# Feed-forward activations turned on VectorE in 32x32 blocks instead of on TensorE, and one low part per group moved to GpSimd

## The chip, the cores and the metric

The kernel runs on one core of one Trainium2 chip. The time is the device time of one execution in microseconds (us); lower is better. A comparison of this kernel with itself resolves differences of about 0.2%, that is some 6 us.

## What is computed

A block of 256 tokens with 2048 channels goes through feed-forward, token mixing (three kinds of attention), feed-forward again, and then two more layers with four mixers each. Everything is float32. What matters here are the two feed-forward parts:

```python
def _swiglu(h, w_gu, w_down):          # h 256 x 2048, w_gu 2048 x 11264, w_down 5632 x 2048
    gate, up = jnp.split(h @ w_gu, 2, axis=-1)
    return (jax.nn.silu(gate) * up) @ w_down

x = x + 0.5 * _swiglu(_rmsnorm(x, ffn1_norm), ffn1_w_gu, ffn1_w_down)
x = x + _token_mixing(_rmsnorm(x, mix_norm), ...)
x = x + 0.5 * _swiglu(_rmsnorm(x, ffn2_norm), ffn2_w_gu, ffn2_w_down)
```

In the second block each layer also needs `mod = silu(c) @ w_ada + b_ada` for one row `c`, with `w_ada` 2048 x 6144. It does not depend on `x`, and the kernel works it out during the feed-forward parts (called "ada" below).

## The kernel before

**Weights as slabs.** All weights stream from memory in slabs of 512 KB, one after another, in one fixed order that all engines share. SyncE starts the transfers (`load`, L693) into four buffers (`stage`). A float32 weight is used as the sum of two rounded parts: ScalarE writes the high part (`rounded_part`, L1411), and then either VectorE (`slab_lo`, L1830) or GpSimd (`rest`, L777) writes the low part, stage minus high. The set `by_vector` says who makes the low part of which slab. In the feed-forward parts it holds the odd slabs and GpSimd has the even ones. There are four places for split slabs too: ScalarE may round slab n once TensorE has finished slab n-4, and SyncE may load slab n+4 once the low part of slab n is written.

**TensorE** (`wide_passes`) does twelve matmuls of 512 columns on a slab: eight with the high part of the weight (L898), for which it waits for ScalarE, and then four with the low part (L903), for which it waits for VectorE or GpSimd.

**One group** of a feed-forward part is 16 slabs, eight for 512 gate columns and eight for 512 up columns. There are 11 groups (j = 0 to 10) and then 88 slabs of the down projection. Slab q of group j is called (j, q) here. Around a group's end the products are made into the input of the down projection:
- ScalarE, at (j, 11): `silu` of the gate product, from PSUM into the tile SILU (L1472), 128 tokens x 512 channels, twice.
- VectorE, at (j+1, 3): `gated` multiplies by the up product (L1876, two instructions).
- TensorE, after (j+1, 2): `turn_act` turns the tile with eight 128x128 transposes (L816) into PSUM banks 6 and 7, since the down projection needs channels on partitions.
- ScalarE, at (j+1, 6): `round_act` writes the high part of the turned tile (L1478, two instructions).
- VectorE, at (j+1, 7): `rest_act` writes the low part (L1884, two instructions). The down projection waits for `act_lo`.

For j = 10 these steps fall in the first slabs of the down projection, which stand in as a group 11.

**Order on VectorE.** Every engine goes through its own list in order. VectorE's list at a slab is: the low part if the slab is its own, then `ada_pick` if due, then one `ada` step if due, then `rest_act` or others. An ada step (L1843 or L1840, then L1846) adds two rows of `w_ada` chunks of 512 columns; there are 96 of them in each feed-forward part, one on every 2.4 slabs from slab 18 to slab 245. After each eighth one TensorE sums over partitions (`ada_reduce`, L957), one slab later, and VectorE picks the result (`ada_pick`, L1857 and L1858), one more slab later. So at a pick VectorE stands still until TensorE has come to that very slab. By `ADA_AT` the picks fall on (2, 4), (3, 7), (4, 11), (5, 14), (7, 1), (8, 4), (9, 7), (10, 10) and (11, 14), and three later in the down projection.

## Time and profile before

| | |
|---|---|
| time, median of 3 runs | 3107.89 us (3107.75 to 3108.13) |
| span of the profiled execution | 3105.2 us |
| TensorE busy | 3070.2 us, 99% |
| VectorE busy | 1952.8 us, 63% |
| ScalarE busy | 1447.7 us, 47% |
| GpSimd busy | 1270.0 us, 41% |
| TensorE clock granted | full in all 40 slices |

The profile is one execution seen by the hardware profiler. Its span is 2.7 us below the median time, since the time also counts what lies before the first and after the last instruction. A busy time contains the time in which an instruction has started and is held up. The chain is followed back from the last instruction to whatever released each step. The first feed-forward part runs from the start to about 755 us, the second from about 1475 to 2214 us.

### The profile page before, as it was taken

What the parts mean: (1) busy time and instruction counts of PE and PEld (TensorE: products, weight loads), DVE (VectorE), ACT (ScalarE), POOL (GpSimd) and SP (SyncE); (2) the same over time, 40 slices, a digit from 0 to 9 for tenths busy, and PEclk for the clock granted to TensorE, in tenths of its full rate; (3) what the DMA queues carried; (4) which work ended last, traced back from release to release, by engine and by line L of the source; (5) the groups of instructions that cost most, each with busy time, mean ns of one, the idle gap of its engine ahead of it and who ended that gap; (6) DMA issues with size and microseconds to landing.
All of it is one profiled execution on the core that took longest, in us unless ns stands there. A gap on an engine that the chain in (4) does not pass through costs nothing.

```text
span 3105.2 us, 46479 instructions
## 1 busy us (share of the span) xinstructions
PE 3070.2 (99%) x19038; PEld 2713.0 (87%) x19038; DVE 1952.8 (63%) x2398; ACT 1447.7 (47%) x1877; POOL 1270.0 (41%) x621
## 2 busy tenths in 40 slices
PE   8999999999999999999999999999999999999998
PEld 7888888888999999998888888888899998899986
DVE  5778576673323446773467667677469864589764
ACT  6444444444567545544544444344444454544444
POOL 4444444444566554584444444444610004510013
PEclk9999999999999999999999999999999999999999
DMA  7878777785776565565787778787666545565454
GB/s 230 284 245 282 260 268 268 252 283 175 218 177 181 156 168 145 150 172 195 237 270 257 273 252 276 244 290 246 191 181 190 158 142 199 166 191 178 155 166 166
DMA packets 486653, 662.74 MB, mean 213 GB/s; under 512 B 67992, under 2 KB 273544, under 8 KB 486184
## 3 DMA queue, kind: packets, MB, share of 16 engines
q1 hardware_dynamic: 480952, 655.05, 66.1%
q0 software_dynamic: 4448, 2.94, 0.4%
q8 instruction: 150, 2.46, 0.3%
q10 hardware_dynamic: 1040, 1.78, 0.2%
q14 instruction: 63, 0.52, 0.1%
HBM read 655.47 MB, written 2.10 MB: 212 GB/s over the span
## 4 chain that ended last, share of the span: by engine, by line
PE 97%; DVE 1%; ACT 1%; issue 0%; DMA 0%; POOL 0%; ACTq 0%; DVEq 0%
PE ps L898 36%; PE ps L826 23%; PE ps L903 18%; PE ps L832 11%; PE ps L816 2%; PE ps L857 1%; PE ps L1356 1%; PE ps L1144 1%; PE ps L1125 1%; PE ps L957 0%; PE ps L1052 0%; PE ps L1152 0%; PE ps L1182 0%; PE ps L1174 0%; PE ps L1191 0%
## 5 line engine op out<-in xcount | busy, mean ns | idle before, releaser
L777 POOL TENSOR_TENSOR split_slabs<-stage,split_slabs 128x1024 fp32r<-128x1024 f32 x296 | 749.8, 2534 | 1365.6 <-ACT split_slabs L1411 1365.6
L1411 ACT ACTIVATE split_slabs<-stage 128x1024 fp32r<-128x1024 f32 x592 | 627.6, 1062 | 903.7 <-PE ps L903 665.1
L898 PE MATMUL ps<-split_slabs,h_split 128*128 128x512 f32 x3312 | 827.1, 392 | 0.9 <-ACT split_slabs L1411 0.9
L1411 ACT ACTIVATE narrow_split_slabs<-stage 128x1024 fp32r<-128x1024 f32 (+1 forms) x440 | 461.0, 1052 | 651.2 <-PE ps L832 568.1
L826 PE MATMUL ps<-h_split,narrow_split_slabs 128*128 128x256 f32 x5856 | 748.4, 280 | 0.0
L898 PEld LDWEIGHTS ps<-split_slabs,h_split 128*128 128x128 f32 x3312 | 620.8, 188 | 133.8 <-issue 5.1
L826 PEld LDWEIGHTS ps<-h_split,narrow_split_slabs 128*128 128x128 f32 x5856 | 702.8, 188 | 15.7 <-issue 12.0
L1830 DVE TENSOR_TENSOR split_slabs<-stage,split_slabs 128x1024 fp32r<-128x1024 f32 x296 | 412.2, 1395 | 368.2 <-ACT split_slabs L1411 368.1
L777 POOL TENSOR_TENSOR narrow_split_slabs<-stage,narrow_split_slabs 128x1024 fp32r<-128x1024 f32 (+1 forms) x181 | 436.0, 2418 | 315.0 <-ACT narrow_split_slabs L1411 307.3
L1830 DVE TENSOR_TENSOR narrow_split_slabs<-stage,narrow_split_slabs 128x1024 fp32r<-128x1024 f32 x259 | 333.1, 1288 | 175.8 <-ACT narrow_split_slabs L1411 174.9
L903 PE MATMUL ps<-split_slabs,h_split 128*128 128x512 f32 x1656 | 443.0, 389 | 0.3 <-POOL split_slabs L777 0.3
L832 PE MATMUL ps<-h_split,narrow_split_slabs 128*128 128x256 f32 x2928 | 397.8, 278 | 1.6 <-POOL narrow_split_slabs L777 1.4
L903 PEld LDWEIGHTS ps<-split_slabs,h_split 128*128 128x128 f32 x1656 | 310.9, 188 | 65.9 <-POOL split_slabs L777 0.7
L832 PEld LDWEIGHTS ps<-h_split,narrow_split_slabs 128*128 128x128 f32 x2928 | 364.2, 188 | 2.6 <-POOL narrow_split_slabs L777 2.0
L898 PE MATMUL ps<-split_slabs,act_split 128*128 128x512 f32 x1392 | 344.6, 390 | 0.0
L898 PEld LDWEIGHTS ps<-split_slabs,act_split 128*128 128x128 f32 x1392 | 260.9, 188 | 54.2
L1843 DVE SCALAR_TENSOR_TENSOR U<-U,cact 128x512 f32<-128x512 f32 x168 | 213.6, 1271 | 5.1 <-DMA U<-in_w_ada 4.7
L1846 DVE SCALAR_TENSOR_TENSOR U<-U,cact 128x512 f32<-128x512 f32 x192 | 201.3, 1048 | 6.8
L903 PE MATMUL ps<-split_slabs,act_split 128*128 128x512 f32 x696 | 186.1, 389 | 0.0
L903 PEld LDWEIGHTS ps<-split_slabs,act_split 128*128 128x128 f32 x696 | 130.6, 188 | 27.4
L1857 DVE TENSOR_TENSOR ps<-ps,base_consts 128x512 f32<-128x512 f32 x24 | 16.8, 700 | 162.1 <-PE ps L957 162.1
L2191 DVE SCALAR_TENSOR_TENSOR U<-U,params 128x256 f32<-128x256 f32 x240 | 110.8, 503 | 0.0
(250 smaller groups left out, 2129.4 us busy)
## 6 DMA issues: line engine op xcount, KB each, us to landing
stage<-in_w_in SPq DMA_DIRECT2D x360, 512.0 KB, 3.7
stage<-in_ffn_w_gu SPq DMA_DIRECT2D x352, 512.0 KB, 4.8
U<-in_w_ada SPq DMA_DIRECT2D x192, 512.0 KB, 5.6
stage<-in_ffn_w_down SPq DMA_DIRECT2D x176, 512.0 KB, 5.6
stage<-in_w_out SPq DMA_DIRECT2D x96, 512.0 KB, 4.1
stage<-in_w_in SPq DMA_DIRECT2D x80, 128.0 KB, 2.9
stage<-in_w_branch_c SPq DMA_DIRECT2D x32, 192.0 KB, 3.3
stage<-in_cmp_w SPq DMA_DIRECT2D x8, 512.0 KB, 5.8
```

The source lines that it names most:

```text
L777: nc.gpsimd.tensor_tensor(slab_part(n, 1, size(n)), stage[:, n % RING, 0:size(n)], slab_part(n, 0, size(n)).bitcast(F32), ALU.subtract).th ...
L816: return nc.tensor.transpose(dst, src, ident[0:n, 0:n])
L826: mm(bank[:, c * S:(c + 1) * S], w[0][:, kk, at:at + P], moving(kk, i), start=first and c == 0 and kk == 0 and i == 0, stop=False)
L832: ins = mm(bank[:, c * S:(c + 1) * S], w[1][:, kk, at:at + P], moving(kk, 0), start=False, stop=last and c == outs - 1 and kk == chunks - 1)
L857: ins = mm(acc(g)[:, c * S:(c + 1) * S], w[:, kk, c * P:(c + 1) * P], hx[:, i, KC * k + kk, :], start=first and c == 0 and kk == 0, stop=l ...
L898: mm(ps[:, 2 * pair + T, :], stationary(kk, i)[:, T * P:(T + 1) * P], w[0][:, kk, :], start=first and kk == 0 and i == 0, stop=False)
L903: ins = mm(ps[:, 2 * pair + T, :], stationary(kk, 0)[:, T * P:(T + 1) * P], w[1][:, kk, :], start=False, stop=last and kk == WK - 1)
L1411: return fn(slab_part(n, 0, size(n)), stage[:, n % RING, 0:size(n)], ACT.Copy)
L1830: v.tensor_tensor(slab_part(n, 1), stage[:, n % RING, :], slab_part(n, 0).bitcast(F32), ALU.subtract).then_inc(lo_vec, 1)
L1843: ins = v.scalar_tensor_tensor(total, w[:, 0, :], cact[:, 2 * k:2 * k + 1], total, ALU.mult, ALU.add)
L1846: v.scalar_tensor_tensor(total, w[:, 1, :], cact[:, 2 * k + 1:2 * k + 2], total, ALU.mult, ALU.add).then_inc(ada_load, 1)
L2191: ins = v.scalar_tensor_tensor(cy[:, c, :], src, col, cy[:, c, :], ALU.mult, ALU.add)
```

## The change

The eight transposes and the PSUM banks go away. VectorE turns the tile itself: a vector transpose works inside blocks of 32x32, and here each instruction reads 32 partitions (one quadrant `a`) and writes 32 partitions (quadrant `b`), 256 elements on each, so that 16 instructions place all blocks where a full transpose needs them. They are put on VectorE's list four at a time, at (j+1, 4) to (j+1, 7). The turned tile lies where the low part will be; ScalarE rounds it from there in one instruction of 1024 elements, at (j+1, 10), and VectorE writes the low part over it in one instruction, at (j+1, 11). TensorE no longer waits for anything of this. Slab (j, 5) of the groups 1 to 11 goes from VectorE to GpSimd.

```diff
+        def turned_act(j):
+            return u(AT - SHIFT + FC * S + 4 * j * S, P, 4 * S)
...
+        by_vector -= {s + 16 * j + 5 for s in (S_F1, S_F2) for j in range(1, GU_GROUPS + 1)}
...
-            def turn_act(f, j):
-                at = GU_GROUPS * f + j
-                pe.wait_ge(evacuated, (G_F1, G_F2)[f] + j + 1)
-                if at == 0:
-                    pe.wait_ge(*vec_out.after("par", len(PARAM_TILES) - 1))
-                if at > 0:
-                    pe.wait_ge(act_lo, at)
-                for c in range(4):
-                    for T in range(TT):
-                        last = transpose(ps[:, 6 + c // 2, (c % 2) * S + T * P:(c % 2) * S + (T + 1) * P],
-                                         u(SILU, P, TT, WN)[:, T, c * P:(c + 1) * P])
-                last.then_inc(act_turned, 1)
...
-                            if side == 0 and q == 2 and j > 0:
-                                turn_act(f, j - 1)
...
             def round_act(f, j):
                 act.wait_ge(act_turned, GU_GROUPS * f + j + 1)
-                for k in range(2):
-                    fn(ats[:, 0, (4 * j + 2 * k) * S:(4 * j + 2 * k + 2) * S], ps[:, 6 + k, :], ACT.Copy).then_inc(act_hi, 1)
+                part = slice(4 * j * S, 4 * (j + 1) * S)
+                fn(ats[:, 0, part], turned_act(j), ACT.Copy).then_inc(act_hi, 1)
...
-                        if j > 0 and q == 6:
+                        if j > 0 and q == 10:
                             round_act(f, j - 1)
...
+                def turn_act(j, a):
+                    rows = slice(a * SQUARE, (a + 1) * SQUARE)
+                    src = u(SILU, P, TT, WN).rearrange("p t (c w) -> p t c w", c=4)
+                    dst = turned_act(j).rearrange("p (c t s) -> p t c s", c=4, t=TT)
+                    if a == 0:
+                        dve.wait_ge(evacuated, g0 + j + 1)
+                    for b in range(P // SQUARE):
+                        turned_rows = slice(b * SQUARE, (b + 1) * SQUARE)
+                        last = v.transpose(dst[turned_rows, :, :, rows], src[rows, :, :, turned_rows])
+                    if a == P // SQUARE - 1:
+                        last.then_inc(act_turned, 1)
+
                 def rest_act(j):
-                    at = GU_GROUPS * f + j
-                    for k in range(2):
-                        part = slice((4 * j + 2 * k) * S, (4 * j + 2 * k + 2) * S)
-                        dve.wait_ge(act_hi, 2 * at + k + 1)
-                        last = v.tensor_tensor(ats[:, 1, part], ps[:, 6 + k, :], ats[:, 0, part].bitcast(F32), ALU.subtract)
-                    last.then_inc(act_lo, 1)
+                    part = slice(4 * j * S, 4 * (j + 1) * S)
+                    dve.wait_ge(act_hi, GU_GROUPS * f + j + 1)
+                    v.tensor_tensor(ats[:, 1, part], turned_act(j), ats[:, 0, part].bitcast(F32), ALU.subtract
+                                    ).then_inc(act_lo, 1)
...
-                        if j > 0 and q == 7:
+                        if j > 0 and 4 <= q < 8:
+                            turn_act(j - 1, q - 4)
+                        if j > 0 and q == 11:
                             rest_act(j - 1)
```

## Rows read from the trace of the kernel before

**Rows 1.** The page: busy times, and the chain that ended last by engine.
```profile
PE 3070.2 (99%) x19038; PEld 2713.0 (87%) x19038; DVE 1952.8 (63%) x2398; ACT 1447.7 (47%) x1877; POOL 1270.0 (41%) x621
...
PE 97%; DVE 1%; ACT 1%; issue 0%; DMA 0%; POOL 0%; ACTq 0%; DVEq 0%
```
**Rows 2.** Chain in order of time: start us, us, what; around one turning, first part.
```profile
67.07 1.81 PE ps L898 x8
68.88 0.91 PE ps L903 x4
69.79 0.87 PE ps L816 x8
70.67 1.84 PE ps L898 x8
```
**Rows 3.** Timeline of TensorE (start us, us, what) around the turning in group 7.
```profile
337.81 1.07 PE L903 MATMUL ps<-split_slabs,h_split 128*128 128x512 f32 x4
339.01 1.09 PE L816 MATMUL ps<-base_consts,U 128*128 128x128 f32 x8
```
**Rows 4.** Single lines, whole span: count, shortest/median/longest ns, first and last start.
```profile
L1884 DVE TENSOR_TENSOR act_split<-ps,act_split x44: 676/681/687, 77.0 to 1988.0; 128x512 fp32r<-128x512 f32 x44
...
L1830 DVE TENSOR_TENSOR split_slabs<-stage,split_slabs x296: 1207/1224/3457, 27.5 to 3086.5; 128x1024 fp32r<-128x1024 f32 x148
...
L1843 DVE SCALAR_TENSOR_TENSOR U<-U,cact x168: 735/746/2978, 69.6 to 2156.1; 128x512 f32<-128x512 f32 x168
...
L1840 DVE TENSOR_SCALAR U<-U,cact x24: 476/481/2625, 62.1 to 2117.1; 128x512 f32<-128x512 f32 x24
...
L2273 DVE COPY U<-ps x16: 412/418/422, 2377.9 to 2987.4; 128x256 f32<-128x256 f32 x16
...
L777 POOL TENSOR_TENSOR split_slabs<-stage,split_slabs x296: 2375/2402/3495, 11.6 to 3082.9; 128x1024 fp32r<-128x1024 f32 x148
```
**Rows 5.** Timelines of VectorE and GpSimd in group 7.
```profile
340.79 2.77 DVE L1846 SCALAR_TENSOR_TENSOR U<-U,cact 128x512 f32<-128x512 f32 x1
...
346.06 1.22 DVE L1830 TENSOR_TENSOR split_slabs<-stage,split_slabs 128x1024 fp32r<-128x1024 f32 x1
347.20 1.28 DVE L1884 TENSOR_TENSOR act_split<-ps,act_split 128x512 fp32r<-128x512 f32 x2
...
340.40 2.62 POOL L777 TENSOR_TENSOR split_slabs<-stage,split_slabs 128x1024 fp32r<-128x1024 f32 x1 [3.83 <-ACT split_slabs L1411]
347.06 2.48 POOL L777 TENSOR_TENSOR split_slabs<-stage,split_slabs 128x1024 fp32r<-128x1024 f32 x1 [4.05 <-ACT split_slabs L1411]
```
**Rows 6.** Busy time of each engine in stretches from one turning to the next.
```profile
115.10:160.00 44.90, 44.90 (x203) 37.21 (x203) 36.77 (x35) 18.98 (x21) 20.49 (x8) 1.00 0.84 285
...
340.10:384.50 44.40, 44.40 (x202) 36.82 (x201) 27.16 (x28) 19.02 (x21) 19.77 (x8) 1.00 0.86 294
...
sum 448.60, PE 448.47 PEld 371.50 DVE 322.96 ACT 190.78 POOL 204.35; mean PE 44.85 PEld 37.15 DVE 32.30 ACT 19.08 POOL 20.44
```
**Rows 7.** What VectorE waited for from 60 to 550 us: total us, times, longest.
```profile
DVE split_slabs L1830 <- ACT split_slabs L1411: 71.8, 33, 4.4
DVE ps L1857 <- PE ps L957: 60.4, 9, 8.5
```
**Rows 8.** Timeline of VectorE and chain of TensorE after the pick at (2, 4).
```profile
118.34 0.70 DVE L1857 TENSOR_TENSOR ps<-ps,base_consts 128x512 f32<-128x512 f32 x1 [4.85 <-PE ps L957]
...
122.00 1.22 DVE L1830 TENSOR_TENSOR split_slabs<-stage,split_slabs 128x1024 fp32r<-128x1024 f32 x1
...
127.92 1.22 DVE L1830 TENSOR_TENSOR split_slabs<-stage,split_slabs 128x1024 fp32r<-128x1024 f32 x1
...
126.51 1.81 PE ps L898 x8
...
131.95 1.81 PE ps L898 x8
```

More of the change, by code:

```diff
@@ L44 @@
 SHIFT = 16
+SQUARE = 32
 GU_GROUPS, DOWN_GROUPS = FF // WN, D // WN
@@ L1015, in ffn @@
                             wide_passes(PAIR[g1 + d], n, act_, q == 0, q == DOWN - 1)
-                        if d == 0 and q == 2:
-                            turn_act(f, GU_GROUPS - 1)
                         if f == 0 and d > 0 and q == 6:
@@ L1512, in ffn_act @@
                     round_upto(s0 + GU_SLABS + i)
-                    if i == 6:
+                    if i == 10:
                         round_act(f, GU_GROUPS - 1)
@@ L1928, in ffn_vec @@
                     between(GU_SLABS + i)
-                    if i == 7:
+                    if 4 <= i < 8:
+                        turn_act(GU_GROUPS - 1, i - 4)
+                    if i == 11:
                         rest_act(GU_GROUPS - 1)
```

## The prediction, made before the changed kernel was run

> **What bounds the kernel now.** I read the page first: busy times, then the chain that ended last. TensorE is busy 99% of the span and holds 97% of the chain [rows 1]. The reader should see that nothing else carries weight: as long as the low and high parts of the slabs come in time, the time is the sum of what TensorE is given, and whatever is taken off it comes off the time. The second view is the chain in order of time around one turning. A slab is 1.81 + 0.91 = 2.72 us, and between two slabs stand 0.87 us of transposes [rows 2]. The third question is what keeps the slabs coming. For that I read the stretches from one turning to the next, the waits of VectorE, and the timelines of VectorE and GpSimd side by side [rows 4 to 8].
>
> **What is removed.** 22 turnings (11 in each feed-forward part) go from TensorE. Each costs 0.87 us, and the eight matmuls behind it take 1.84 instead of 1.81 us [rows 2], so 0.90 us each: 22 x 0.90 = 19.8 us, all on the path. In group 7 the turning started late as well: the four matmuls before it started at 337.81, so it was due 0.91 us later [rows 2], at 338.72, and started at 339.01 [rows 3]. It waited for `gated`. That happens in both parts, since the order is the same: 2 x 0.3 = 0.6 us, also gone. Sum: 20.4 us. The two PSUM banks that come free are used by nobody else here, and TensorE's clock is at full in every slice, so it gives or costs nothing.
>
> ScalarE rounds 1024 elements in one instruction instead of two of 512: nothing, it is busy 19 of 45 us [rows 6]. If its wait for `act_turned` comes late, the high parts of slabs (j, 11) and (j, 12) and the next `silu` are queued behind it; this is taken up below.
>
> **What is added on VectorE.** The trace shows no vector transpose. The nearest row for one instruction is a copy of 256 elements, one input, at 418 ns [rows 4]. Two independent instructions overlap by some 0.08 us (two of 681 ns in 1.28 us [rows 4, 5]), so the bounds for the pace are 0.34 us (they overlap) and, if a transpose takes two cycles for an element, the 418 ns plus once more the difference that 256 elements make: 681 - 418 = 263 ns, so 0.70 us. I take 0.45 us, no overlap: 1.8 us for each of the four parts and 7.2 us a group (bounds 5.5 and 11.2). The Trainium skill (VectorE: DVE Perf Modes, "Two Vector instructions with no wait between them") says that an instruction whose output starts in another quadrant than the last output is held until all earlier ones have finished. Every one of these sixteen writes another quadrant than the one before; by that rule the pace is the 0.45 us, and without it 0.34 us; no row here has such a pair.
>
> Off VectorE's list come one low part in a group, 1.13 us where its neighbours follow at once, and the old `rest_act`, 1.28 us; the new one is one instruction of 1024 elements from SBUF, 1.2 us. Net +6.0 us a group. GpSimd gets one more low part of 2.4 us [rows 4], 9 instead of 8 in a group, 21.6 of 44 us. Slabs 4, 5 and 6 are then all its own; one comes every 2.72 us and takes 2.40, so it keeps up if it is not held.
>
> **What of this is covered.** Idle time on VectorE is 44.85 - 32.30 = 12.6 us a group on average, but only 8.1 us in the stretch from 115 us, and 17 us in the one from 340 us [rows 6]. So 6 us fit on average. But two things make the cover thinner than it looks. First, of 138 idle us about 60 stand before a pick [rows 7]. They are lead that is thrown away: at a pick VectorE meets TensorE at the same slab and has to rebuild its lead. Second, VectorE and GpSimd exclude each other. A scalar_tensor_tensor with two inputs in SBUF, normally 0.75 us, took 2.77 us because GpSimd had started 0.4 us before it, and ended just after GpSimd did; while `rest_act` of before, with one input in PSUM, ran straight through a GpSimd instruction in 1.28 us for two [rows 5]. The longest and shortest times say the same for the whole span: 676 to 687 ns for L1884, but up to 3457 and 2978 ns for L1830 and L1843, and GpSimd's own up to 3495 [rows 4]. The new `rest_act` reads two inputs from SBUF and joins those that can be held.
>
> So I follow the list after a pick. TensorE needs the low part of slab n 1.81 us after the slab's start. At (2, 4): the low part of slab 7 was ready at 123.2 and needed at 126.51 + 1.81 = 128.3, margin 5.1; that of slab 9 at 129.1 and 133.8, margin 4.6 [rows 8]. In the new order three parts of the turning come before slab 7 and the low part of slab 5 is gone: 5.4 - 1.1 = 4.3 later, margin 0.8. Before slab 9 come four parts, and `rest_act` is gone: 7.2 - 1.1 - 1.3 = 4.8 later, margin -0.2. At (7, 1): the low part of slab 7 was ready at 347.3 [rows 5] and needed at 340.10 + 4 x 2.72 + 1.81 = 352.8; 4.3 later, and needed 1.2 us earlier since the turning and its wait are gone from before it: margin 0.0. Each can be hit by one GpSimd instruction, 0 to 2.4 us. ScalarE's rounding of the turned tile comes about 5 us into slab 7 in such a group, and the high part of slab 11 behind it has some 2 us to spare. I give each of these places half a GpSimd instruction, 1.2 us. They are (2, 4), (7, 1) and (8, 4) in each of the two parts, six places: 7.2 us. The picks at slab 7 (groups 3 and 9) change little, as 1.8 us replaces the old 1.28 us there, and the other groups keep margins of 1 to 3 us: together 0.6 us. Sum of new stalls 7.8 us, between 0 and, with a full GpSimd instruction and a negative margin at each place and half that in four others, 6 x 2.6 + 4 x 1.2 = 20 us.
>
> The sum: 3105.2 - 20.4 + 7.8 = 3092.6 us of span, and with the 2.7 us around it 3095.3 us, against a median of 3107.9.
>
> **The rivals.** *The cover holds:* the transposes overlap at 0.34 us, so that every margin above grows by over 1 us, and the collisions fall elsewhere. For it: in the group from 340 us VectorE has 17 idle us. Against: the margins of slabs 7 and 9. Time: 3107.9 - 20.4 = 3087.5.
>
> *The stalls eat the gain:* 20 us of stalls as bounded above, 3107.5. For it: GpSimd's extra 2.4 us falls on just the stretch where VectorE is behind, and GpSimd and VectorE together had little free time in the stretch from 115 us, 36.8 + 20.5 us of 44.9 with what they wait for each other [rows 6]. Against: a stall of TensorE gives all others that time, so it can't repeat at once.
>
> *The transpose is slow and VectorE becomes the bound:* at 0.70 us the turning takes 11.2 us a group, 4.0 more. The six margins fall by 3 to 4 us each, 6 x 3.5 = 21 us, and those of 1 to 3 us in some ten other groups turn to stalls of about 1 us: 3095.3 + 31 = 3126. It decides from about 0.55 us for an instruction.
>
> *The transpose takes part in the exclusion:* this is the one on the other side with the greatest price. The instruction has one input, in SBUF. The tensor_scalar L1840 has also one, does 512 elements in 481 ns, clearly more than an element in the time that L1843 needs for one (746 ns), and it too was held up to 2625 ns [rows 4]. If the transpose is such a fast form, time that can't be shared in a group is GpSimd 9 x 2.4 = 21.6, low parts 7 x 1.1, ada 6.7 x 1.2 (0.75 less some 0.15 in which an instruction is only starting, twice), 1 for its split, 1.1 for `rest_act` and 5 for the transposes: 44.4 us of the 43.9 that a group would have, before any wait for each other. With the 5 us that neither uses in front of the picks, a group is some 4 us longer, over 20 groups 80 us: 3167. It decides if the sixteen together take over about 3 us of the shared time. The Trainium skill (SBUF — State Buffer, "Who interferes with whom") lists copy, cast and tensor_scalar as forms that take the shared ports, and says that a VectorE instruction with at most one SBUF input outside these modes does not contend; transposes are not in its list. L1840 and L1884 here agree with both halves of it, and no row has a transpose; by the rule this rival falls away.
>
> **How the numbers follow.** Some stalls, 3095.3: 0.52. Cover holds, 3087.5: 0.17. Stalls eat the gain, about 3102 to 3110: 0.13. Slow transpose, 3126: 0.10. Exclusion, 3167: 0.08. About 0.2% (6 us) is what a measurement can tell, so faster means below 3101.7. Faster 0.69, same 0.13, slower 0.18. The range holds the first three: from 3086 (all of the 20.4 us and a little rounding) to 3112.
>
> **What would show it.** L816 falls from 614 to 438 instructions and the chain around slab (j, 2) runs 2.72 us after 2.72 us. The transposes are 352 in two stretches, with a mean near 0.42 us; about 0.3 with a longest over 2 means the exclusion, 0.7 the slow one. Right if the waits of TensorE show a few us in total for low parts by VectorE or GpSimd, at slabs 7 and 9 after the picks in groups 2, 7 and 8, and VectorE's busy time in a group rises from 32 to about 39 us. Wrong if these waits are near nothing (cover holds) or appear in all groups.

## The result, and the profile after

The changed kernel takes 3115.45 us (median of 20 runs, 3106.57 to 3125.36) where the kernel before takes 3108.01 us (20 runs, 3102.73 to 3112.01): ratio 1.0025, with a 95% interval of 1.0018 to 1.0031. Forecast were 3095.3 us and a range up to 3112. The median lies above the range, and the sign is wrong. The profiled execution is one of 3111.67 us, with a span of 3109.8 us, against 3105.2 before.

The page of the kernel after, busy times and shares of the chain by engine:

```profile
PE 3056.2 (98%) x18862; PEld 2695.1 (87%) x18862; DVE 2151.5 (69%) x2706; ACT 1445.6 (46%) x1855; POOL 1354.0 (44%) x643
...
PE 89%; DVE 7%; issue 1%; DMA 1%; ACT 1%; POOL 0%; ACTq 0%; DVEq 0%
```

Against [rows 1], TensorE is busy 14 us less and still the bound, but the chain is now 7% VectorE: there are places where TensorE stands and VectorE is what it stands for. TensorE's waits in the feed-forward parts (us in total, times, longest):

```profile
PE ps L910 <- DVE split_slabs L1819: 17.6, 10, 3.8
PE ps L964 <- DVE ada_split L1839: 0.8, 1, 0.8
```

L910 is the four matmuls with the low part, and L1819 the low part by VectorE. Such a wait comes right after eight matmuls with the high part. The first is in group 1, in which there is no pick. TensorE's timeline there (start, length, line, operation, count, idle time before it with its releaser):

```profile
79.44 1.98 PE L905 MATMUL ps<-split_slabs,h_split 128*128 128x512 f32 x8
84.36 1.71 PE L910 MATMUL ps<-split_slabs,h_split 128*128 128x512 f32 x4 [2.95 <-DVE split_slabs L1819]
85.87 3.10 PE L905 MATMUL ps<-split_slabs,h_split 128*128 128x512 f32 x8
88.80 1.07 PE L910 MATMUL ps<-split_slabs,h_split 128*128 128x512 f32 x4
```

Two things cost time here. TensorE is idle for 2.95 us, and the twelve matmuls after it run from 84.36 to 88.80, 4.44 us, where a slab's twelve took 2.72 before [rows 2]. Why the second is so shows in the window over them (length; busy time of PE, PEld, DVE, ACT and POOL with counts; granted clock of TensorE; DMA share; GB/s):

```profile
84.40:87.00 2.60, 2.60 (x7) 2.06 (x8) 2.53 (x5) 0.84 (x1) 0.00 (x0) 0.58 0.56 117
...
50.00:100.00 50.00, 47.05 (x203) 38.30 (x202) 42.31 (x45) 22.14 (x25) 26.13 (x10) 0.97 0.70 237
200.00:250.00 50.00, 47.09 (x200) 38.29 (x199) 44.49 (x50) 19.20 (x19) 22.60 (x10) 0.97 0.68 230
350.00:400.00 50.00, 47.09 (x196) 38.42 (x195) 37.78 (x43) 20.25 (x20) 24.02 (x10) 0.93 0.78 269
1800.00:1850.00 50.00, 45.55 (x193) 36.90 (x192) 48.10 (x49) 18.88 (x20) 23.51 (x9) 0.97 0.74 254
```

After the stall the granted clock is at the lower of its two levels (1.2 instead of 2.4 GHz), here for 3.4 us and in the window from 350 us for 6.8. In this execution it followed each of the four stalls of 2.9 us or more (at 84, 225, 362 and 1822 us), and none of the shorter ones, of which the longest is 2.41 us. Other runs show that the length of the stall alone doesn't decide it. In slab5_back (below) the clock fell behind a stall of 2.39 us and not behind one of 3.18 us; these are the windows right after the two:

```profile
178.00:182.00 4.00, 4.00 (x12) 3.13 (x11) 3.83 (x8) 1.06 (x1) 0.00 (x0) 0.57 0.77 249
...
565.00:572.00 7.00, 6.52 (x28) 5.36 (x29) 5.15 (x8) 2.12 (x2) 0.12 (x1) 1.00 0.48 151
```

The cost in the kernel after is read from the windows of 50 us around its four long stalls, the share of the clock that was not granted times their length: (0.03 + 0.03 + 0.07 + 0.03) x 50 = 8 us.

**Where the time went.** I cut each trace at the same three instructions: the first matmul of the mixing, the first wide one of the second feed-forward part, the last of that part.

| us | first feed-forward | mixing | second feed-forward | two layers |
|---|---|---|---|---|
| before | 755.2 | 723.4 | 735.5 | 891.1 |
| after | 764.0 | 724.5 | 734.4 | 886.9 |

The two feed-forward parts together grew by 7.7 us, although 20.4 us of work was taken off them (below this is measured to be right). So 28.1 us came in: 18.4 in waits, 8 by the clock, and 1.7 not placed. The last column differs by up to 8 us between runs whose code there is the same (886.9 us here, 895 in before_log_later), so the feed-forward columns tell more than the total.

**What holds VectorE.** Its timeline in group 1 ahead of that stall, and GpSimd's:

```profile
65.72 3.19 DVE L1819 TENSOR_TENSOR split_slabs<-stage,split_slabs 128x1024 fp32r<-128x1024 f32 x1
...
68.84 2.88 DVE L1832 SCALAR_TENSOR_TENSOR U<-U,cact 128x512 f32<-128x512 f32 x1
71.76 2.78 DVE L1835 SCALAR_TENSOR_TENSOR U<-U,cact 128x512 f32<-128x512 f32 x1
74.46 3.57 DVE L1879 STREAM_TRANSPOSE U<-U 32x256 f32<-32x256 f32 x8
...
79.62 1.78 DVE L1879 STREAM_TRANSPOSE U<-U 32x256 f32<-32x256 f32 x4
81.42 2.89 DVE L1819 TENSOR_TENSOR split_slabs<-stage,split_slabs 128x1024 fp32r<-128x1024 f32 x1
```

```profile
65.44 2.39 POOL L784 TENSOR_TENSOR split_slabs<-stage,split_slabs 128x1024 fp32r<-128x1024 f32 x1 [2.02 <-ACT split_slabs L1400]
68.36 5.62 POOL L784 TENSOR_TENSOR split_slabs<-stage,split_slabs 128x1024 fp32r<-128x1024 f32 x2 [0.53 <-ACT split_slabs L1400]
...
80.88 2.35 POOL L784 TENSOR_TENSOR split_slabs<-stage,split_slabs 128x1024 fp32r<-128x1024 f32 x1 [3.08 <-ACT split_slabs L1400]
```

Both halves of an ada step, 0.75 us each when free, take 2.88 and 2.78 us, each together with a GpSimd instruction. Two holds in a row cost 4.2 us, the transposes come that much later, and the low part at 81.42, late already, is held once more (2.89 us instead of 1.22): TensorE gets it 2.95 us late. Over the whole span (count: shortest/median/longest in ns; stretch):

```profile
L1879 DVE STREAM_TRANSPOSE U<-U x352: 422/436/443, 74.5 to 2004.8; 32x256 f32<-32x256 f32 x176
L1832 DVE SCALAR_TENSOR_TENSOR U<-U,cact x168: 734/747/2906, 68.8 to 2164.9; 128x512 f32<-128x512 f32 x168
L1835 DVE SCALAR_TENSOR_TENSOR U<-U,cact x192: 750/752/2955, 63.7 to 2165.6; 128x512 f32<-128x512 f32 x192
L1819 DVE TENSOR_TENSOR split_slabs<-stage,split_slabs x274: 1208/1224/3426, 26.5 to 3091.1; 128x1024 fp32r<-128x1024 f32 x137
L1886 DVE TENSOR_TENSOR act_split<-U,act_split x22: 1215/1221/3434, 93.4 to 2009.0; 128x1024 fp32r<-128x1024 f32 x22
L1970 DVE TENSOR_SCALAR U<-U x8: 181/181/2280, 153.0 to 253.2; 128x32 f32<-128x32 f32 x8
L1969 DVE TENSOR_TENSOR U<-U x8: 187/192/2391, 152.7 to 253.0; 128x32 f32<-128x32 f32 x8
```

The transposes are never held and never slow. Held are, of these rows, the instructions with two inputs in SBUF and the `tensor_scalar`. L1886 is the new `rest_act`. The rows of L1969 and L1970 were not in my working at all: they belong to `log_sigmoid`, a small part of the mixing that VectorE makes ahead of time in groups 2 to 6 of the first feed-forward part, at (j, 1). They take 0.19 us, and when held up to 2.4.

The kernel before has such holds too, with nearly as much time in them. These are the first instruction of an ada step in the kernel before and in the kernel after (busy us, mean ns), against a median of 0.75 us in both:

```profile
L1843 DVE SCALAR_TENSOR_TENSOR U<-U,cact 128x512 f32<-128x512 f32 x168 | 213.6, 1271 | 5.1 <-DMA U<-in_w_ada 4.7
```

```profile
L1832 DVE SCALAR_TENSOR_TENSOR U<-U,cact 128x512 f32<-128x512 f32 x168 | 225.0, 1339 | 11.3 <-DMA U<-in_w_ada 10.7
```

So the holds are not new. What is new is that TensorE has to wait behind some of them.

### The profile page after: what moved, and what is told of

Same layout as the page of the kernel before. It is cut to its first block, busy times and chain, and to the rows that moved or that the text cites. A ratio compares the mean times of both kernels' runs of the same rounds, so it can differ in the third digit from the quotient of the medians.

```text
span 3109.8 us, 46413 instructions
## 1 busy us (share of the span) xinstructions
PE 3056.2 (98%) x18862; PEld 2695.1 (87%) x18862; DVE 2151.5 (69%) x2706; ACT 1445.6 (46%) x1855; POOL 1354.0 (44%) x643
## 4 chain that ended last, share of the span: by engine, by line
PE 89%; DVE 7%; issue 1%; DMA 1%; ACT 1%; POOL 0%; ACTq 0%; DVEq 0%
PE ps L905 31%; PE ps L833 23%; PE ps L910 16%; PE ps L839 11%; PE ps L823 2%; DVE split_slabs L1819 1%; DVE U L1832 1%; DVE U L1879 1%; PE ps L864 1%; DVE U L1835 1%; PE ps L1345 1%; PE ps L1133 1%; PE ps L1114 1%; POOL narrow_split_slabs L784 0%; DMA stage<-in_ffn_w_gu 0%
## 5 line engine op out<-in xcount | busy, mean ns | idle before, releaser
L784 POOL TENSOR_TENSOR split_slabs<-stage,split_slabs 128x1024 fp32r<-128x1024 f32 x318 | 834.7, 2628 | 1283.9 <-ACT split_slabs L1400 1283.6
L1819 DVE TENSOR_TENSOR split_slabs<-stage,split_slabs 128x1024 fp32r<-128x1024 f32 x274 | 406.5, 1486 | 238.5 <-ACT split_slabs L1400 237.7
L910 PE MATMUL ps<-split_slabs,h_split 128*128 128x512 f32 x1656 | 447.5, 392 | 16.3 <-DVE split_slabs L1819 16.0
L1819 DVE TENSOR_TENSOR narrow_split_slabs<-stage,narrow_split_slabs 128x1024 fp32r<-128x1024 f32 x259 | 332.3, 1285 | 171.4 <-ACT narrow_split_slabs L1400 170.1
L910 PEld LDWEIGHTS ps<-split_slabs,h_split 128*128 128x128 f32 x1656 | 311.9, 189 | 85.3 <-DVE split_slabs L1819 19.7
L1832 DVE SCALAR_TENSOR_TENSOR U<-U,cact 128x512 f32<-128x512 f32 x168 | 225.0, 1339 | 11.3 <-DMA U<-in_w_ada 10.7
L1835 DVE SCALAR_TENSOR_TENSOR U<-U,cact 128x512 f32<-128x512 f32 x192 | 221.7, 1155 | 6.8
L910 PE MATMUL ps<-split_slabs,act_split 128*128 128x512 f32 x696 | 186.5, 390 | 1.6 <-DVE split_slabs L1819 1.6
L1879 DVE STREAM_TRANSPOSE U<-U 32x256 f32<-32x256 f32 x352 | 153.2, 435 | 5.3
L910 PEld LDWEIGHTS ps<-split_slabs,act_split 128*128 128x128 f32 x696 | 130.4, 188 | 30.0 <-DVE split_slabs L1819 2.9
```

The lines of the kernel that those rows point to most:

```text
L784: nc.gpsimd.tensor_tensor(slab_part(n, 1, size(n)), stage[:, n % RING, 0:size(n)], slab_part(n, 0, size(n)).bitcast(F32), ALU.subtract).th ...
L910: ins = mm(ps[:, 2 * pair + T, :], stationary(kk, 0)[:, T * P:(T + 1) * P], w[1][:, kk, :], start=False, stop=last and kk == WK - 1)
L1819: v.tensor_tensor(slab_part(n, 1), stage[:, n % RING, :], slab_part(n, 0).bitcast(F32), ALU.subtract).then_inc(lo_vec, 1)
L1832: ins = v.scalar_tensor_tensor(total, w[:, 0, :], cact[:, 2 * k:2 * k + 1], total, ALU.mult, ALU.add)
L1835: v.scalar_tensor_tensor(total, w[:, 1, :], cact[:, 2 * k + 1:2 * k + 2], total, ALU.mult, ALU.add).then_inc(ada_load, 1)
L1879: last = v.transpose(dst[turned_rows, :, :, rows], src[rows, :, :, turned_rows])
```

## The experiments

Each ratio is to runs of the kernel before on the same chip, with its 95% interval.

### Is GpSimd's extra low part the cause?

**slab5_back**, the kernel after with slab (j, 5) given back to VectorE:

```diff
-        by_vector -= {s + 16 * j + 5 for s in (S_F1, S_F2) for j in range(1, GU_GROUPS + 1)}
```

> The changed kernel with one part undone: the low part of slab (j, 5) goes back from GpSimd to VectorE; the transposes stay on VectorE. Theory X (the stalls come from VectorE being held by GpSimd, and the extra GpSimd instruction makes slabs 4, 5 and 6 one row of three holds just where the turning is): the waits of TensorE for low parts by VectorE fall from 17.6 us to under 6 us, and the time to 3092 to 3100 us. Theory Y (the stalls come from the turning's own 7.2 us on VectorE's list; GpSimd is incidental): VectorE has 1.1 us more in front of slab 7, so the waits are 17 us or more and the time 3113 to 3125 us.

Measured: 3122.89 us (3121.56 to 3125.98, 5 runs), ratio 1.0046 (1.0034 to 1.0058). TensorE's wait for the low parts by VectorE:

```profile
PE ps L909 <- DVE split_slabs L1818: 23.9, 19, 3.9
```

The waits grow from 17.6 to 23.9 us, as theory Y expected. I had seen the extra GpSimd instruction as the one that VectorE meets; it is a relief of about 7 us: without it VectorE has 1.2 us more on its list in front of slab 7.

**slab5_alone**, the kernel before with that one line added.

> The kernel before, with only the low part of slab (j, 5) given to GpSimd; the transposes stay on TensorE. Theory X: the row of three GpSimd instructions by itself eats most of the margin of slabs 7 and 9, TensorE waits 4 to 10 us in total for low parts, 3112 to 3120 us. Theory Y: VectorE has less to do, no waits, 3108 us as before (within 2).

Measured: 3106.97 us (3102.55 to 3112.49, 11 runs), ratio 0.9995 (0.9987 to 1.0004). Alone, this half of the change does nothing. It does give holds in a row, as theory X said. In group 1 of slab5_alone:

```profile
70.59 2.89 DVE L1844 SCALAR_TENSOR_TENSOR U<-U,cact 128x512 f32<-128x512 f32 x1
73.51 2.77 DVE L1847 SCALAR_TENSOR_TENSOR U<-U,cact 128x512 f32<-128x512 f32 x1
```

Ada steps with both halves held (over 1.3 us each, one right behind the other) are found 20 times in the feed-forward parts of slab5_alone, 10 times in the kernel after, and never in the kernel before or in slab5_back. They come with GpSimd's extra low part. But slab5_alone has them and no stall, and slab5_back has none and more waits, so they are not what decides.

### What is the removed work worth, and does VectorE's extra time eat it?

**four_wide_turns**, the kernel after with four transposes over 128 partitions instead of sixteen over 32 (it leaves out the moves between quadrants):

```diff
-                    for b in range(P // SQUARE):
-                        turned_rows = slice(b * SQUARE, (b + 1) * SQUARE)
-                        last = v.transpose(dst[turned_rows, :, :, rows], src[rows, :, :, turned_rows])
+                    last = v.transpose(dst[:, :, :, rows], src[:, :, :, rows])
```

> The changed kernel with the sixteen transposes of a turning replaced by four over all 128 partitions (each turns the blocks inside every quadrant, so the blocks do not move between quadrants: this part of the computation is left out). VectorE has 1.8 instead of 7.2 us for a turning, all else is as in the changed kernel, GpSimd's extra low part too. Both theories: 3087 to 3090 us if the removal from TensorE is worth the 20.4 us that was worked out. Theory X in its strong form (the row of three GpSimd instructions is enough) expects 4 to 8 us of waits left, 3092 to 3098 us; theory Y none.

Measured: 3087.61 us (3084.32 to 3091.76, 5 runs), ratio 0.9935 (0.9923 to 0.9948). TensorE's waits for low parts by VectorE, the first turning on VectorE's timeline, and the same row of the ada steps as above:

```profile
PE ps L910 <- DVE split_slabs L1819: 0.9, 2, 0.5
...
68.92 2.88 DVE L1832 SCALAR_TENSOR_TENSOR U<-U,cact 128x512 f32<-128x512 f32 x1
71.84 2.77 DVE L1835 SCALAR_TENSOR_TENSOR U<-U,cact 128x512 f32<-128x512 f32 x1
74.53 0.76 DVE L1877 STREAM_TRANSPOSE U<-U 128x256 f32<-128x256 f32 x2
...
75.96 2.77 DVE L1835 SCALAR_TENSOR_TENSOR U<-U,cact 128x512 f32<-128x512 f32 x1
...
L1832 DVE SCALAR_TENSOR_TENSOR U<-U,cact 128x512 f32<-128x512 f32 x168 | 255.1, 1518 | 15.8 <-DMA U<-in_w_ada 15.3
```

The feed-forward parts take 744.4 + 726.0 = 1470.4 us, 20.3 less than before: the 20.4 us of the forecast are all there once VectorE has 5.5 us a group less to do. The granted clock in them is at full. So the whole loss comes through VectorE's list. The holds are all still there: the same two in front of the first turning, one more behind it, and a mean of 1518 ns for the ada instruction, more than the 1339 of the kernel after. Held this much, VectorE still keeps up when the turning is 5.5 us shorter. The stalls need the length of the turning as well as the holds.

### Ada steps away from the turning, and log-sigmoid away from the groups

**ada_aside**, the kernel after with no ada step on slabs 3 to 7 of a group:

```diff
-ADA_AT = [18 + m * 230 // ADA_LOADS for m in range(ADA_LOADS)]
+ADA_FREE = [i for i in range(18, 249) if not (i < 16 * 12 and 3 <= i % 16 <= 7)]
+ADA_AT = [ADA_FREE[m * (len(ADA_FREE) - 3) // (ADA_LOADS - 1)] for m in range(ADA_LOADS)]
```

> The changed kernel with the ada steps moved: none falls on slabs 3 to 7 of the groups 1 to 11, so nothing stands on VectorE's list there but gated, the turning and the low parts of slabs 3 and 7. About 3 us (two steps, more when held) leave the stretch in front of slab 7. Both theories expect fewer stalls; X, for which each ada step is two chances to be held for up to 2.4 us, expects nearly none, 3088 to 3094 us; Y expects about half of them left, 3098 to 3106 us.

Measured: 3112.06 us (3099.7 to 3116.01, 12 runs), ratio 1.0005 (0.9994 to 1.0015), which neither theory had expected. The waits are still 15.2 us, but two of them, 5.09 and 4.67 us, stand right behind `log_sigmoid`, at slab 3 of the groups 3 and 5 (in this order group 5 also has a pick at slab 1). VectorE and GpSimd of this kernel in group 3:

```profile
151.92 0.19 DVE L1970 TENSOR_TENSOR U<-U 128x32 f32<-128x32 f32 x1
152.14 2.36 DVE L1971 TENSOR_SCALAR U<-U 128x32 f32<-128x32 f32 x1
154.54 0.19 DVE L1970 TENSOR_TENSOR U<-U 128x32 f32<-128x32 f32 x1
154.76 2.33 DVE L1971 TENSOR_SCALAR U<-U 128x32 f32<-128x32 f32 x1
157.13 2.32 DVE L1970 TENSOR_TENSOR U<-U 128x32 f32<-128x32 f32 x1
159.49 2.25 DVE L1971 TENSOR_SCALAR U<-U 128x32 f32<-128x32 f32 x1
...
154.64 7.06 POOL L785 TENSOR_TENSOR split_slabs<-stage,split_slabs 128x1024 fp32r<-128x1024 f32 x3 [0.18 <-ACT split_slabs L1401]
```

Four holds in six instructions. As long as GpSimd has low parts waiting, each of VectorE's tiny instructions that can be held may meet another GpSimd instruction. The price of such a step on VectorE's list is therefore not its length alone, but also how many times it gives way.

**log_later**, the kernel after with `log_sigmoid` in the down projection instead (slabs 74 to 82, its scratch tile in memory of its own):

```diff
-                        if f == 0 and 2 <= j < 7 and q == 1:
-                            log_sigmoid(j - 2)
...
+                    if f == 0 and 74 <= i < 84 and i % 2 == 0:
+                        log_sigmoid(i // 2 - 37)
```

> The changed kernel with the log-sigmoid of the decay logits moved: some thirty VectorE instructions of 32 elements, 0.19 us each, at (2, 1) to (6, 1) of the first feed-forward part, go to slabs 74 to 82 of its down projection, where no ada step and no turning is left (their scratch gets a place of its own). Theory Z (VectorE stalls TensorE where it is behind, and each instruction with SBUF operands, however short, is then held for a whole GpSimd instruction): the stalls of the first part become like those of the second, 764 us for it become 752 to 757, and the time 3103 to 3109 us. Rival (short instructions do not matter, their own 6 us over five groups is all): first part 760 to 763, time 3112 to 3115.

Measured: 3107.76 us (3101.21 to 3114.93, 11 runs), ratio 0.9995 (0.9984 to 1.0006); the first feed-forward part falls from 764.0 to 754.6 us, and the waits from 17.6 to 12.2 us. The stalls of 2.41 and 2.91 us at slab 7 of the groups 3 and 4 are gone, each with a `log_sigmoid` at slab 1 of its group before. So this explains 9 us (0.30% between the two ratios), and why the first part suffered more than the second.

**before_log_later**, the kernel before with the same move.

> The kernel before with the same move of the log-sigmoid and nothing else. All theories: no stall of TensorE depends on it, 3106 to 3110 us, as the kernel before.

Measured: 3110.44 us (3103.93 to 3113.86, 11 runs), ratio 0.9996 (0.9987 to 1.0005). Before the change `log_sigmoid` cost nothing where it stood; only with the turning on VectorE does it cost something.

**ada_aside_log_later**, both moves in the kernel after.

> Both moves: ada steps off the slabs 3 to 7, log-sigmoid in the down projection. With the ada steps moved the two stalls of 5 us that were left in the first part each stood behind a log-sigmoid whose short instructions were held 2.3 us apiece. Theory Z: each part is then 4 to 7 us shorter than before the change, 3094 to 3101 us, waits of TensorE for VectorE under 6 us. Rival (VectorE is simply full and the stall comes elsewhere): 3104 to 3110.

Measured: 3098.45 us (3096.88 to 3102.72, 5 runs), ratio 0.9963 (0.995 to 0.9975). **two_slabs_more** gives GpSimd slab (j, 9) as well:

```diff
-        by_vector -= {s + 16 * j + 5 for s in (S_F1, S_F2) for j in range(1, GU_GROUPS + 1)}
+        by_vector -= {s + 16 * j + q for q in (5, 9) for s in (S_F1, S_F2) for j in range(1, GU_GROUPS + 1)}
```

> As the one with both moves, and the low part of slab (j, 9) given to GpSimd as well. If VectorE's own load is what is left (slab 5 on VectorE had cost 7 us): 3088 to 3095 us. If GpSimd's holds weigh as much as the load they relieve: no better, 3096 to 3102.

Measured: 3102.47 us (3096.84 to 3107.56, 9 runs), ratio 0.9976 (0.9967 to 0.9986). The waits of the two kernels, first ada_aside_log_later:

```profile
PE ps L912 <- DVE split_slabs L1821: 5.5, 11, 1.4
```

and two_slabs_more:

```profile
PE ps L912 <- DVE split_slabs L1821: 10.0, 13, 3.0
```

With both moves no stall is longer than 1.4 us, and the clock of the feed-forward parts is at full; the feed-forward parts take 1482.1 us, 8.6 less than before. One low part more to GpSimd gains nothing. Whether it costs something isn't shown: the two intervals overlap, and its profile is of the slowest of its nine runs.

**before_ada_aside_log_later** is the control, the kernel before with both moves.

> The kernel before (transposes on TensorE) with the two moves of the version at 3098 us: ada steps off the slabs 3 to 7 of the groups, log-sigmoid in the down projection. If the gain of that version comes from taking the transposes off TensorE: 3108 to 3116 us here (nothing to gain from the moves; a few us lost where the down projection has more ada steps, as the waits at 600 to 690 us there showed). If the moves gain by themselves: below 3103.

Measured: 3118.26 us (3110.93 to 3122.86, 9 runs), ratio 1.0032 (1.0021 to 1.0043). In this order of the work the turning change, with its extra low part, is worth 1.0032 - 0.9963 = 0.69% or 21 us, all that was forecast for the removal. The order itself costs the kernel before 10 us, a little more than was expected (up to 3116 us).

### Does the order of the ada steps cost by itself?

Three kernels with `log_sigmoid` moved and the ada steps at fixed slabs of each group: **ada_even_log_later** (from after), **ada_even_slab5_back** (the same with slab 5 given back) and **before_ada_even_log_later** (from before).

```diff
-ADA_AT = [18 + m * 230 // ADA_LOADS for m in range(ADA_LOADS)]
+ADA_SLOTS = (0, 1, 8, 10, 11, 13, 15)
+ADA_AT = [i for i in range(18, 16 * 12) if i % 16 in ADA_SLOTS]
+ADA_AT += [16 * 12 + 1 + m * 54 // (ADA_LOADS - len(ADA_AT)) for m in range(ADA_LOADS - len(ADA_AT))]
```

> The changed kernel with the log-sigmoid in the down projection and the ada steps on fixed places of each group, seven at slabs 0, 1, 8, 10, 11, 13 and 15 of the groups 1 to 11 and the other 21 evenly over the down projection. In the version before it nine of sixteen slabs of the down projection's first part had an ada step and most of the waits that were left stood there. If VectorE's momentary backlog is what sets the waits: under 3 us of waits for low parts, 3090 to 3097 us. If not, as there, 3098 (3096 to 3101).

> The same with the low part of slab (j, 5) back on VectorE. In the changed kernel that step cost 7 us. If it is VectorE's own load against the margin of slabs 7 and 9, the margin is now 3 us and more, since no ada step stands there, and 1.1 us of it does no harm: within 3 us of the run beside it. If GpSimd's extra instruction is a relief at any place: 5 to 8 us slower again.

> The kernel before (transposes on TensorE) with the same two moves. TensorE never waited for low parts there, so the moves can gain nothing: 3107 to 3111 us, as the kernel before. If it came out below 3103, the gain of the other runs would be the moves' own and not that of taking the transposes off TensorE.

Measured: 3138.51 us (6 runs), ratio 1.0096 (1.0079 to 1.0112); 3139.4 (6 runs), 1.0093 (1.0078 to 1.0107); 3143.79 (5 runs), 1.0108 (1.0094 to 1.0121). All three are some 30 us slower than the kernel before and miss what was expected, the one from before as well, so it isn't the turning. SyncE's queue points to the cause (before_ada_even_log_later):

```profile
SPq L705 <- DVE U L1849: 415.8, 113, 10.5
```

and the kernel before:

```profile
SPq L702 <- DVE U L1846: 97.3, 63, 6.1
```

The loads of ada weights and of slabs go through one queue in one order. An ada load waits for one of two buffers. The reading is that with two steps on neighbouring slabs it waits longer, and the slab loads behind it wait too. By `ADA_AT` there are 31 such pairs here and none in the kernel before; the order of ada_aside has 16, and its cost in the kernel before was 10 us. These three say nothing on the holds.

**ada_every_second** takes the pairs away:

```diff
-ADA_AT = [18 + m * 230 // ADA_LOADS for m in range(ADA_LOADS)]
+ADA_AT = [i for i in range(18, 16 * 12) if i % 16 in (0, 2, 8, 10, 12, 14)]
+ADA_AT += [16 * 12 + 1 + m * 62 // (ADA_LOADS - len(ADA_AT)) for m in range(ADA_LOADS - len(ADA_AT))]
```

> The changed kernel with the log-sigmoid in the down projection and ada steps never on neighbouring slabs: slabs 0, 2, 8, 10, 12 and 14 of each group, then every second slab of the down projection. The version with pairs (10 and 11; 15, 0 and 1) lost 30 us with and without the turning on VectorE. If pairs are what was wrong there: 3093 to 3099 us. If any fixed list that keeps slabs 3 to 7 free and is denser elsewhere loses: 3110 or more.

Measured: 3112.78 us (3107.8 to 3117.12, 11 runs), ratio 1.0011 (1.0003 to 1.002). Most of the 30 us are gone with the pairs (this order also has six instead of seven steps in a group, so the pairs are not the only difference). The time is in the range of the second expectation, though it is slower than log_later by only some 5 us. It has five stalls, four of 3.0 us and one of 2.6. The four stand in the groups 5 and 9 of both parts, at the low part of slab 3, one slab behind the picks of this order on (5, 2) and (9, 2). So here the lead that is lost at a pick does show.

### The same work on VectorE without the holds of the ada steps

If the stalls need the holds, they must go when VectorE does the same work without being held. [rows 5] show how: an instruction with an input in PSUM runs through a GpSimd instruction. **ada_sum_in_psum** is the kernel after with the running sum of the ada steps in PSUM bank 5, which is free in these parts (the squares of the norm, whose output nobody reads, go to SBUF there):

```diff
-                w, total = u(ADA_RING, P, 2, WK, WN)[:, m % 2], u(ADA_ACC + WN, P, WN)
+                w, total = u(ADA_RING, P, 2, WK, WN)[:, m % 2], ps[:, 5, :]
...
```

> The changed kernel with the running sum of the ada steps in PSUM bank 5 instead of SBUF (ScalarE's unused squares go to SBUF for that). Each ada instruction then has one SBUF input and takes the same time by itself. Theory E (what breaks VectorE's margins is being held by GpSimd through two-input SBUF instructions): the 360 ada instructions, median 0.75 us and longest 2.9 us before, now all take under 0.8 us, VectorE's busy time falls by 60 to 150 us, waits of TensorE for low parts by VectorE fall from 17.6 us to under 6, time 3092 to 3100 us. Theory L (it is the own length of the list): ada instructions are not shorter in the median, waits stay above 12 us, time 3110 to 3118 us.

Measured: **3087.66 us (3086.96 to 3091.1, 5 runs), ratio 0.9929 (0.9916 to 0.9941)**, faster than both kernels. Its page, its ada steps and the window from 60 to 550 us:

```profile
PE 3049.4 (99%) x18862; PEld 2694.5 (87%) x18862; DVE 1934.9 (63%) x2706; ACT 1445.0 (47%) x1855; POOL 1316.9 (43%) x643
...
L1833 DVE SCALAR_TENSOR_TENSOR ps<-U,cact,ps x168: 704/749/758, 67.0 to 2139.6; 128x512 f32<-128x512 f32 x168
L1836 DVE SCALAR_TENSOR_TENSOR ps<-U,cact,ps x192: 754/756/758, 63.0 to 2140.4; 128x512 f32<-128x512 f32 x192
...
60.00:550.00 490.00, 489.76 (x2159) 404.95 (x2158) 370.11 (x495) 209.21 (x209) 255.20 (x101) 1.00 0.80 270
```

and the same window of the kernel after, then of the kernel before:

```profile
60.00:550.00 490.00, 477.70 (x2072) 392.34 (x2071) 439.03 (x483) 203.47 (x202) 263.03 (x98) 0.99 0.77 262
```

```profile
60.00:550.00 490.00, 489.87 (x2204) 405.86 (x2203) 347.25 (x334) 207.37 (x218) 225.66 (x89) 1.00 0.79 267
```

The same 2706 instructions on VectorE are busy 2151.5 - 1934.9 = 217 us less. The medians of these two rows differ by 4 ns at most from those of the kernel after, so nearly all of it was time in which instructions stood. No ada step goes above 758 ns. The picks, the log-sigmoid, the turning and GpSimd's list are where they were in the kernel after, and yet in the window TensorE is idle for 0.2 us, at full clock. The feed-forward parts take 1470.6 us, 20.1 less than before. Theory E forecast too little: it had 60 to 150 us for VectorE and 3092 to 3100 us.

Taken with four_wide_turns: less length with all the holds ends the stalls, and so does the full length without the holds of the ada steps. The kernel before has the holds without the length, and no stall. So each of the two is needed, and neither alone is the cause.

**late_picks** adds the remedy that my forecast pointed to: the pick ten slabs after the last step of its eight, instead of two (and the wait for it moved to the eighth step of the next).

```diff
-ADA_SUM, ADA_PICK = 1, 2
+ADA_SUM, ADA_PICK = 1, 10
...
-                    dve.wait_ge(ada_red, ADA_GROUPS * f + b)
+                    dve.wait_ge(ada_split_done, ADA_GROUPS * f + b)
...
+                    if ADA_GROUPS * f + b >= 1:
+                        dve.wait_ge(ada_red, ADA_GROUPS * f + b)
```

> As the one beside it, and VectorE no longer meets TensorE at a pick: the pick stands ten slabs after the last ada step instead of two, and the wait for TensorE's sum is moved from the first ada step of the next eight to the last. Tests the claim of the prediction that lead is thrown away at the picks. If it is: VectorE's waits for L964 (162 us in the kernel before) vanish, TensorE's waits for VectorE fall by another 2 us or more, 3088 to 3094 us. If lead was not short any more: equal to the run beside it within 2 us.

Measured: 3090.65 us (3088.24 to 3090.93, 5 runs), ratio 0.9934 (0.9921 to 0.9946). VectorE no longer waits at picks, and nothing is gained: 3.0 us more than the run beside it, with intervals that overlap. Once the holds of the ada steps are gone, the lead lost at picks is not needed. Late picks with the holds left in place were not run.

**late_picks_log_later** moves `log_sigmoid` too, and **before_late_picks_log_later** makes all three changes to the kernel before.

> All three: running sum in PSUM, late picks, log-sigmoid in the down projection. If any stall is left behind short held instructions it goes: 3087 to 3091 us, the time without stalls; no granted clock below full in the feed-forward parts.

> The kernel before (transposes on TensorE) with the same three edits. TensorE waited for nothing there but 0.3 us twice at the start of a turning, so 3106 to 3110 us; below 3103 would mean that the edits gain by themselves and not by what they allow.

Measured: 3088.06 us (3084.88 to 3089.94, 5 runs), ratio 0.9927 (0.9915 to 0.9939); and 3109.69 us (3105.95 to 3111.55, 11 runs), 0.9997 (0.9988 to 1.0006). The kernel before gains nothing from any of it, because it had no stalls to lose. Between these two the change under study is worth 0.7%, the 20 us of the removal.

## Why the prediction was wrong

**The bound: right.** The stalls of TensorE and the work taken off it show in the time.

**The removal, 20.4 us: right.** Measured with the stalls away: 20.3 (four_wide_turns) and 20.1 us (ada_sum_in_psum), in the lengths of the feed-forward parts.

**The price of a transpose, 0.45 us: right.** Eight in 3.57 us, 0.446 each; and they take no part in the exclusion. The rivals of the slow transpose and of the exclusion fall with that.

**VectorE's busy time in a group, 32 to about 39 us: right.** 347.25 and 439.03 us in 490 are 31 and 39 in a group of 44, 8 more where +6.0 was worked out. The rest fits the greater time in holds. In this window 69 us, 6 of the 39 in a group, go when the ada steps aren't held (370.11 us). The kernel before had most of such holds already, inside its 32.

**The new stalls, 7.8 us: this is the step that failed.** The mechanism, a list that is longer and is held by GpSimd, was the right one; the term was too small. The waits measure 18.4 us, more than twice the 7.8 and just inside the bound of 20; with 8 us by the clock and 1.7 not placed 28.1 us came in. By place (us of TensorE's waits for VectorE's low parts, both parts together):

| | group 2 | group 7 | group 8 | all others |
|---|---|---|---|---|
| forecast | 2.4 | 2.4 | 2.4 | 0.6 |
| measured | 0 | 7.7 | 0 | 9.9 |

Of the 9.9 us, 8.3 are the three stalls in the groups 1, 3 and 4, for which next to nothing was allowed. Half a GpSimd instruction at six fixed places was the wrong form for this term: most places were spared, and those that were hit lost far more than 1.2 us. Three things lay behind it:

- *Holds that come in rows.* "I give each of these places half a GpSimd instruction, 1.2 us" takes one meeting for each place. In the trace they come in rows: 2.88, 2.78 and 2.89 us in group 1, four in six instructions of `log_sigmoid` in ada_aside. In group 1 the two in front of the turning made it 4.2 us late, and the margin there was to be 1 to 3 us. The row that could have told me was there: L1843 with up to 2978 ns [rows 4] said that an ada instruction can take four times its length, and there are two in a step. slab5_alone and four_wide_turns took such rows without a stall: they break a margin only where the turning has used it up.
- *Which instructions.* I listed what the change moves, and left out `log_sigmoid`, which stays where it is and lost its cover. With 0.19 us for an instruction it looked like nothing; moving it away was worth 9 us in the kernel after and nothing in the one before.
- *The clock.* I wrote that the clock "gives or costs nothing", and took a stall to cost its own length. Each of the four stalls of 2.9 us or more was followed by 3.4 or 6.8 us at half clock, 8 us over the two parts. That is a term that I had put at nothing, and with it the 18.4 us of waits go over the bound of 20.

**The places: half right.** I named the slabs behind the picks in groups 2, 7 and 8. Group 7 has its stall in both parts, at 362 and 1822 us, both at the low part of slab 7 as worked out. Groups 2 and 8 have none. Those at 84, 178 and 225 us, in groups 1, 3 and 4 of the first part, were not on my list; they too stand at the low part of slab 7, and the last two groups carry `log_sigmoid`. What the lead lost at the picks adds is not settled. ada_sum_in_psum keeps the picks and has no stall, so it makes none by itself; but the stalls of group 7, and those of ada_every_second in the groups 5 and 9, stand right behind picks.

**GpSimd's extra low part: the wrong sign.** I counted it as what VectorE collides with. It relieves the changed kernel by about 7 us, and does nothing to the one before.

**The rival "the stalls eat the gain"** named the right mechanism and said against itself that a stall "gives all others that time, so it can't repeat at once". It did not need to repeat at once: ten separate waits were enough. Its 3102 to 3110 us were still too low: 3107.9 - 20.4 + 18.4 gives 3105.9, and it takes the 8 us by the clock, which was in neither sum, to come near what was measured.

## What to carry to other kernels

Where two engines exclude each other, a step that is added to one of them has two prices: its length, which uses up margin even if it is never held itself, and what the holds around it then break, one whole instruction of the other engine each time and several in a row. Go through everything that stays near it on that list, the tiny instructions too. Either side can be the remedy: here a turning 5.5 us shorter (as a test only) and ada steps that aren't held each gave the 20 us of the removal. If an operand of the instructions that are held can live in PSUM, try that: here it turned a change that lost 0.25% into one that gains 0.7%. And half clock can follow a stall of TensorE of two or three us (3.4 or 6.8 us of it here, so 1.7 or 3.4 us on top of the stall), so a few long stalls can cost more than many short ones.

## What was not expected of the hardware

- One operand in PSUM exempts an instruction of VectorE with two inputs from the exclusion: at most 758 ns over 360 instructions, against up to 2955 with both in SBUF. The Trainium skill (SBUF — State Buffer, "Who interferes with whom") says that a VectorE instruction with two SBUF inputs contends with a GpSimd instruction that reads SBUF, and one with at most one outside the shared-port modes doesn't. The traces agree on both, and on the transposes: 422 to 443 ns, one input, never held.
- Two transposes of 256 elements over 128 partitions, whose outputs start at the same partition, took 0.76 us, so the second came 0.33 us after the first. Those over 32 partitions, each to another quadrant than the one before, came every 0.446 us (3.57 for eight). The Trainium skill (VectorE: DVE Perf Modes, "Two Vector instructions with no wait between them") says that an instruction to another quadrant is held until the earlier ones have finished; the numbers agree.
- After a stall of 2.95 us the granted clock was at half for 3.4 us, and eight matmuls took 2.93 instead of 1.81 us. The 2.41 us one, and eleven of at most 1.4 us in ada_aside_log_later, were followed by no such stretch; of slab5_back's, 2.39 us was and 3.18 us wasn't. What decides between them is not shown.
